# Ranked expert weights: whole experts to a slot, in a two-block kernel on one core

## What is computed

```python
def hier_moe(x, rg_w, rg_b, re_w, re_b, w_gate, w_up, w_down):
    t = x.reshape(B * S, D)                      # 256 tokens x 1024
    ...                                          # every token chooses 1 of 4 groups, 2 of its 8 experts
    for g in range(N_GROUPS):
        h = silu(einsum('td,edf->tef', t, w_gate[g])) * einsum('td,edf->tef', t, w_up[g])
        y = y + einsum('tef,efd->td', h * gate[:, g, :, None], w_down[g])
```

## The kernel before

| loads | what |
|---|---|
| B0 to B9 | group 0: gate and up of units 0 to 3 (B0, B1; B2, B3; B4, B5; B7, B8), down(0) B6, down(1) B9 |
| B10, B11; B12 | gate_up(4); down(2) |
| B13, B14; B15 | gate_up(5); down(3) |
| B16 to B19; B20 | gate_up(6); down(4) |
| B21 to B24; B25 | gate_up(7); down(5) |
| B26 to B29; B30, B31 | gate_up(8); down(6) |
| B32 to B35; B36, B37 | gate_up(9); down(7) |
| B38 to B41; B42 to B47 | gate_up(10); down(8), down(9), down(10) |

## Time and profile before

### The profile page before, as it was taken

How to read it: one execution, slowest core, us unless ns; L and a number is a source line. 1 busy time by engine, 2 the same in 40 slices (tenths; PEclk the granted TensorE clock), 3 DMA queues, 4 the chain that set the end, 5 groups by cost and what they waited for, 6 DMA issues and landing times. The chain is left out here.

```text
span 1629.5 us, 18987 instructions
## 1 busy us (share of the span) xinstructions
PE 1352.7 (83%) x7532; PEld 756.1 (46%) x7532; DVE 493.5 (30%) x1148; ACT 298.5 (18%) x621; POOL 0.2 (0%) x4
## 2 busy tenths in 40 slices
PE   6999999856656566599999999766899999998667
PEld 4665877412212211266777644222667677433223
DVE  5125553101101101016653523111247645222103
ACT  2422202000100000112322312100123323122001
POOL 0000000000000000000000000000000000000000
PEclk9999999988877878899999999988999999999888
DMA  9465477999999999992321699999614214999993
GB/s 391 166 246 212 169 295 310 417 429 427 427 428 428 427 428 428 429 413 90 119 104 52 238 399 395 411 409 410 282 64 195 104 52 161 388 401 410 409 409 120
DMA packets 63297, 492.62 MB, mean 302 GB/s; under 512 B 7008, under 2 KB 7392, under 8 KB 39008
## 3 DMA queue, kind: packets, MB, share of 16 engines
q1 hardware_dynamic: 63056, 491.15, 74.2%
q10 hardware_dynamic: 144, 0.13, 0.0%
HBM read 490.21 MB, written 1.05 MB: 301 GB/s over the span
## 5 line engine op out<-in xcount | busy, mean ns | idle before, releaser
L651 PE MATMUL PS<-A 128*128 128x256 f32 (+5 forms) x1568 | 367.6, 392 | 5.3 <-DMA A<-ring_d 1.6
L1007 PE MATMUL PS<-A 128*32 128x512 f32 x1536 | 233.2, 744 | 139.3 <-DMA A<-ring_d 139.3
L651 PEld LDWEIGHTS PS<-A 128*128 128x128 f32 (+1 forms) x1568 | 274.2, 192 | 90.4 <-issue 51.3
L1543 PE MATMUL PS<-A 128*32 128x512 f32 (+1 forms) x1024 | 168.5, 635 | 40.7 <-DMA A<-ranked_d 40.7
L1007 PEld LDWEIGHTS PS<-A 128*32 128x32 f32 x1536 | 52.2, 124 | 306.7 <-issue 241.4
L1572 PE MATMUL PS<-A 128*32 128x512 f32 (+1 forms) x512 | 95.8, 730 | 37.6 <-issue 37.6
L1543 PEld LDWEIGHTS PS<-A 128*32 128x32 f32 (+1 forms) x1024 | 47.1, 124 | 144.6 <-issue 143.6
L2073 DVE TENSOR_TENSOR A<-A,PS 128x512 f32<-128x512 f32 x8 | 5.5, 687 | 320.9 <-PE PS L1007 320.9
L656 PE MATMUL PS<-A 128*128 128x128 f32 (+1 forms) x428 | 63.5, 278 | 17.8 <-DVE A L2073 7.1
L656 PEld LDWEIGHTS PS<-A 128*128 128x128 f32 (+1 forms) x428 | 48.3, 143 | 57.5 <-issue 33.1
L1572 PEld LDWEIGHTS PS<-A 128*32 128x32 f32 (+1 forms) x512 | 26.0, 140 | 103.6 <-issue 103.1
(11 more groups left out here) (389 smaller groups left out, 1278.3 us busy)
## 6 DMA issues: line engine op xcount, KB each, us to landing
A<-ring_d SPq DMA_DIRECT2D x156, 2048.0 KB, 26.2
A<-ranked_d SPq DMA_DIRECT2D x240, 512.0 KB, 14.7
A<-ranked_d SPq DMA_DIRECT2D x24, 1024.0 KB, 8.3
A<-ring_d SPq DMA_DIRECT2D x2, 1312.0 KB, 22.2
A<-ring_d SPq DMA_DIRECT2D x2, 1280.0 KB, 22.4
A<-p_d SPq DMA_DIRECT2D x1, 1232.0 KB, 22.5
A<-xT_d SPq DMA_DIRECT2D x1, 1024.0 KB, 5.3
A<-cT_d SPq DMA_DIRECT2D x1, 1024.0 KB, 11.8
```

The costliest lines, as they stand in the source:

```text
L651: ins = g.matmul(out, l, r, start=n == 0, stop=n == len(pairs) - 1)
L1007: ins = g.matmul(ps[32 * e:32 * e + 32, :], rows_of(kk, e), wv[:, kk % 2, e, :], start=kk == 0, stop=kk == 7)
L1543: ins = g.matmul(ps[m * s:m * s + m, :], XS2[u % 2][:, kk, c:c + m], wv[:, kk % nk, s, :], start=kk == 0, stop=kk == 7)
```

## The change

A slot now holds whole experts. The gate and up weights of one ranked expert are fetched by one DMA of 4096 floats a partition (16 KB rows, 2 MB) into a slot of its own, and the down weights of two whole experts share a slot, two DMAs of 2048 floats (8 KB rows, 1 MB each). `gate_up` splits: group 0's units keep their two parts, ranked units go to `whole_experts`, which waits for all slots of the unit (four, or two) and gives them back together after the last matmul. The order of the matmuls stays, and so do the number of slots, of loads, and the bytes moved.

```diff
             def gate_up(n):
                 (x, j), u = UNITS[n], gather_of(n)
                 ps = high("sg", l, n)
-                parts_, m = (4, 32) if four(n) else (2, 64)
-                for part in range(parts_):
-                    w, i = weights("gr", l, x, j, part) if x else weights("gu", l, n, part)
...
+                if x:
+                    whole_experts(n, ps)
+                    return
+                for part in range(2):
+                    w, i = weights("gu", l, n, part)
...
+            def whole_experts(n, ps):
+
+                (x, j), u = UNITS[n], gather_of(n)
+                m = 32 if four(n) else 64
+                got = [weights("gr", l, x, j, s) for s in range(128 // m)]
+                wv = [w.rearrange("p (k n) -> p k n", k=8) for w, i in got]
+                for d in range(4):
+                    g.wait_ge(*at("xs2", l, u, d // 2, d % 2))
+                for w, i in got:
+                    arrived(i)
+                for kk in range(8):
+                    for s in range(128 // m):
+                        c = (j % 2) * 128 + s * m
+                        ins = g.matmul(ps[m * s:m * s + m, :], XS2[u % 2][:, kk, c:c + m], wv[s][:, kk, :], start=kk == 0, stop=kk == 7)
+                ins.then_inc(*full("sg", l, n))
+                for w, i in got:
                     finished(i)
...
             def down(n):
...
-                if four(n):
-                    wd = [w.rearrange("p (e n) -> p e n", e=4) for w, i in got]
-                else:
-                    wd = [got[0][0].rearrange("p (e f n) -> p f e n", e=2, f=2)[:, f, :, :] for f in range(2)]
+                wd = [w.rearrange("p (e f n) -> p e f n", e=2, f=2) for w, i in got]
...
             def ranked(i, x, kind, l, group_, j, part):
 
                 of = ranks(j) if group_ == 1 else range(4 * (j % 2), 4 * (j % 2) + 4)
-                n = SLOT // len(of)
-                c = n * part + (4096 if kind == "dr" else 0)
+                of, n, c = (of[part:part + 1], SLOT, 0) if kind == "gr" else (of[2 * part:2 * part + 2], SLOT // 2, SLOT)
```

More of the change, by code:

```diff
@@ L1528, in gate_up @@
                 ps = high("sg", l, n)
-                parts_, m = (4, 32) if four(n) else (2, 64)
-                for part in range(parts_):
-                    w, i = weights("gr", l, x, j, part) if x else weights("gu", l, n, part)
-                    nk = 8 // parts_
-                    if x:
-                        wv = w.rearrange("p (s k n) -> p k s n", k=nk, n=512)
-                    else:
-                        wv = w.rearrange("p (k s n) -> p k s n", k=nk, n=512)
-                    for d in range(part * nk // 2, (part + 1) * nk // 2):
+                if x:
+                    whole_experts(n, ps)
+                    return
@@ L1538, in gate_up @@
+                for part in range(2):
+                    w, i = weights("gu", l, n, part)
+                    wv = w.rearrange("p (k s n) -> p k s n", k=4, n=512)
+                    for d in (2 * part, 2 * part + 1):
                         g.wait_ge(*at("xs2", l, u, d // 2, d % 2))
                     arrived(i)
[L1540 to L1543, removed]
@@ L1544, in gate_up @@
-                    ins.then_inc(*(full("sg", l, n) if part == parts_ - 1 else up("pe")))
+                    for kk in range(4 * part, 4 * part + 4):
+                        for s in range(2):
+                            c = (j % 2) * 128 + s * 64
+                            ins = g.matmul(ps[64 * s:64 * s + 64, :], XS2[u % 2][:, kk, c:c + 64], wv[:, kk % 4, s, :], start=kk == 0, stop=kk == 7)
+                    ins.then_inc(*(full("sg", l, n) if part else up("pe")))
+                    finished(i)
@@ L1571, in down @@
                         for s in range(128 // m):
-                            ins = g.matmul(ps[m * s:m * s + m, :], HD[n % 2][:, f, m * s:m * s + m], wd[f][:, s, half * 512:(half + 1) * 512],
+                            ins = g.matmul(ps[m * s:m * s + m, :], HD[n % 2][:, f, m * s:m * s + m], wd[s // 2][:, s % 2, f, half * 512:(half + 1) * 512],
                                            start=f == 0, stop=f == 1)
```

## The result

| | before | changed |
|---|---|---|
| median of 16 runs each | 1631.66 us (1629.16 to 1636.22) | 1627.70 us (1623.53 to 1630.13) |
| ratio, 95% interval | | 0.9969 (0.9960 to 0.9978) |
| profiled execution, span | 1629.5 us | 1626.8 us |
| ranked fetches | 264 | 96 |

0.31% faster, 5.1 us by the ratio. The changed kernel ran three more times beside the kernel before, among the experiments: 0.9979 (0.9965 to 0.9992), 0.9987 (0.9975 to 1.0000) and 0.9970 (0.9957 to 0.9983). The mean of the four is 0.9976, 3.9 us; each of them alone is good to 1.5 to 2.1 us either way. One execution of a later kernel (halves and warm, 1622.78 us) took 4763 us; it stands in that median and not in its ratio.

A forecast was written before the change was run, and what follows sets the result against it. Late in the expert stages the DMA engines were taken as the bound. Per layer 5.1 us gained less 2.3 lost, 2.6 when following every slot, made 5.2 us off the 1632.96 median: 1627.8 us, range 1622 to 1636.

The forecast's parts named there:

- The likeliest case: Whole program: 1627.8 us, 0.32% faster, with its own range of 1625 to 1630 and a chance of 0.46.
- Longer rows: Ranked fetches late in each expert stage: longer rows move at a higher rate, gaining 5.1 us a layer.
- rival (c): Ranked fetches: 409 GB/s even with 16 KB rows, the source setting the rate; 4.6 us slower, 1637.6; chance 0.11.
- The pause before B20: Start of each expert stage's late part: a slot released later leaves the DMA engines 2.3 us late a layer.
- The step that was off: Late part of each expert stage: the DMA engines never stop after the pause before B20; no further pause was booked.
- The signs: Both expert stages: 420 to 428 GB/s over the last 150 us, 96 ranked fetches, last down 2 to 3 us earlier.
- Nothing booked for the cold start: Late gate_ups after idling: 8.6 to 10.0 us fits narrowly within 10.6 to 12.0, so no cost was booked.
- Rival (d): Late gate_ups at low clock throughout take 14.0 us; DMA engines stall at four places, 10 us a layer, 1653; chance 0.07.
- Rival (b): Three places a layer: gate_up near its 10.6 us limit and a thin queue take 3 to 6 us, 1630 to 1634; chance 0.22.
- Rival (a): Expert stages: the queue hides the late release, so 5.1 us a layer stand alone, 1622.7 us; chance 0.14.
- The end: End of each expert stage: TensorE needs 28.4 us at most of 29.9, so the last down still waits for weights.
- SP: Issue of ranked fetches: 168 fewer of 264 gain nothing, since the queue holds SP now and slots will afterwards.

The follow-up runs named there:

- halves and warm: Changed kernel, two-expert units 4 and 5 back to two parts and old fetches, ten idle matmuls before each layer's last down: 1622.78 us, 0.9958; again 1624.84 us, 0.9944.
- 4 KB pieces: Changed kernel, each gate-and-up slot fetched by two DMAs of 128 partitions in alternating 4 KB pieces: 1632.80 us, 1.0010 of the kernel before.
- late release alone: Kernel before with its own fetches, but a ranked gate_up waits for all its slots and gives them back together: 1637.13 us, 1.0023.
- pairs: Kernel of halves and warm, with gate_up of unit 6 in two steps of two slots, given back after each step: 1620.29 us, 0.9925.
- halves: Changed kernel, two-expert units 4 and 5 back to the fetches and two parts of before: 1625.76 us, 0.9953; again 1623.10 us, 0.9934.
- gate_up twice: Changed kernel, gate_up of units 8 to 10 does its 32 matmuls twice into the same bank: 1651.96 us, 1.0138 of the kernel before.

## Why the prediction was right

*The likeliest case came about:* 1627.8 forecast, 1627.7 measured, 5.2 us forecast, 5.1 by that comparison. The two mechanisms, a higher rate late in the stage and a pause from the late release, are both there. But over four comparisons the gain is 3.9, so that the agreement to 0.1 us is luck, and both terms were put too high, which cancels in part.

*Longer rows, 5.1 us a layer* (its terms add up to 5.2). The rates came out nearly as taken: 421 to 431 GB/s, mostly 425 or more, in windows of 16 KB rows at a full DMA share (428 taken) and 417 to 421 with 8 KB (421 taken). So the 24 KB between the rows of ranked_d cost nothing that shows, and rival (c) fell. I had charged the price to the fetch; it belongs to the length of the contiguous piece (4 KB pieces). As every fetch here had one piece a partition the sum was the same. But the gain was not all collected: the changed kernel is only 7.2 us faster than late release alone, 3.6 a layer, or 3.9 by the distances.

*The pause before B20, 2.3 us a layer.* Late release alone cost 1.9 us a layer, and 1.7 us of transfer are missing from 1430 to 1460.

*The step that was off* is that after B20 the DMA engines never stop again. They do, at B23, for gate_up(6) too gives all its slots back at its end. From gate_up(6) to the start of gate_up(8) the changed kernel's four profiles need 46.9 us on average; the kernel before had the last quarter of gate_up(8) start 45.9 us in (1507.62 - 1462.05 = 45.57, and 46.28 in the first layer). So 1.0 us is lost, where 2.3 less the 8 x 0.23 already gained makes 0.5. From there to the last down it is 92.8 before and 89.8 after, 3.0 gained, where 8 x 0.23 + 10 x 0.15 gives 3.3. Together that is 2.1 us a layer for the 2.6 that were forecast, or the 2.8 that the plain terms give: against the plain terms 0.5 us short up to gate_up(8), 0.3 behind it. The second pause fits the 0.5: it ends when gate_up(6) gives its slots back, so that the 2 x 0.23 us saved on B21 and B22 ahead of it only make it longer. That is argued and not shown; no run takes this pause out of the changed kernel alone, pairs does so on top of halves. Some intervals between gate_ups are 30.5 to 31.1 us in place of 29.5 while the mean rate stays at 425 GB/s; the cause of that stays open.

*The signs.* The gate_ups, the single long waits, SP's waits, the 96 fetches and the last down, 3.1 and 3.0 us earlier, came nearly as listed (the waits ahead of the last three gate_ups are 7 to 16 us where 8 to 15 were written). "Over the last 150 us 420 to 428 GB/s" did not: in the four profiles it is 414 to 416 in the first stage and 404 to 409 in the second, for the two pauses and the end of the fetches lie in it; only the inner 90 us (1500 to 1590) have 422 to 424.

*Nothing booked for the cold start.* gate_up took 8.4 to 10.0 us in the changed profiles, 8.6 to 10.0 forecast, against a limit put at 10.6 to 12.0 and measured at 11.7 (gate_up twice). Rival (d) needed 14 us. Rival (b) needed the limit near 10.6 and is gone as a case, though a trace of it shows: behind a gate_up(8) of 9.97 us the window 1516 to 1534 has 417 GB/s at a share of 0.99, behind one of 8.85 us in another profile 431 at 1.02, and gate_up(9) follows after 29.77 us in the first. Rival (a) fell with the pause that the windows at 1435 and 1450 show.

*The end.* The last down waits for its weights as before, 2.7 to 4.1 us behind the group sum. (The profile names no releaser for that wait; the last packets pass up to 1597.0, and it starts at 1597.58.) It took 5.3 us in both layers of the changed profile, where the kernel before had 3.64 and 6.51; 10.7 against 10.2 us in all, so this luck was even.

*SP.* 168 issues fewer gave nothing by themselves, as said: the queue had held SP, now the slots do. No run separates this from the rest.

## What to carry to other kernels

Two numbers decide how to cut a stream of weights into slots: the contiguous piece that a packet can carry (4 KB 408 to 410, 8 KB 417 to 421, 16 KB mostly 425 to 431 GB/s here) and the time at which the reader gives a slot back. Where the transfer is the bound and the reader has time to spare, take the long piece; where the reader is the bound, at the start of a stage, keep small parts and early releases, because a late slot there is a pause: smaller first parts (halves) won 4.2 and 5.9 us over the uniform change. Mixing the two throughout (pairs, with the ten matmuls in it) gained 12 us in the one group that had it, where the uniform change gained 4.9 there and 3.9 on average.

A late release can cost at every unit that has it, and here it did at two. When one pause is taken away, or forecast, look for the next slot that is given back late before calling the rest of the time a bound.

## What I had not expected

A fetch into 32 neighbouring partitions runs at half speed, 215 GB/s with all 16 engines busy, with rows of 16 KB: 251 us for 48 slots cut into strips, and this with the same bytes, and fewer fetches than the kernel before, which runs at 409.

Ten matmuls that bring the last down from 5.21 us or more to 3.64 in both profiles don't show in the timed runs. A profile's clock history is one draw; a gain that rests on it has to be timed.
